# A fused three-block transformer forward on one core: the first norm's root moved behind the first layer, and the last down projection and norm done by token

## The reference, cut to what matters

```python
def rms_norm(x, g):
    xf = x.astype(jnp.float32)
    y = xf * lax.rsqrt(jnp.mean(xf * xf, axis=-1, keepdims=True) + RMS_EPS)
    return y.astype(x.dtype) * g

# first block, layer 0 (the start of the kernel)
hn = rms_norm(h, mix_norm_g[0])
u = hn @ w_pw1 + b_pw1                      # 1024 -> 2048
a, gate = jnp.split(u, 2, axis=-1)
u = a * jax.nn.sigmoid(gate)
u = depthwise_causal_conv(u, w_dw) + b_dw   # 31 taps
u = jax.nn.silu(layer_norm(u, ln_g, ln_b))
h = h + u @ w_pw2 + b_pw2
...
# third block (the end of the kernel)
hf = rmsnorm(x, norm_ffn_g[l])
gate, up = jnp.split(hf @ w_ffn_in[l], 2, axis=-1)      # 1024 -> 2 x 2816
x = x + (jax.nn.silu(gate) * up) @ w_ffn_out[l]         # 2816 -> 1024
return rmsnorm(x, final_norm_g)
```

## Time and profile before

| | |
|---|---|
| Median of 3 runs | 2007.54 us (2007.24 to 2014.68) |
| The profiled execution: its own time | 2004.65 us |
| Its span, first to last instruction | 2002.8 us |
| TensorE busy | 1962.8 us, 98% |
| VectorE busy | 1529.3 us, 76% |
| ScalarE busy | 1214.5 us, 61% |
| Mean granted clock of TensorE | 0.994 |

### The profile page before, as it was taken

The page is one execution under the profiler, slowest core; times in us unless marked ns, Lnnn a source line. Parts: engine busy times, 40 slices in busy tenths (PEclk is TensorE's granted clock), DMA queues, the critical chain, the costliest instruction groups (busy, mean ns, idle before and its releaser), DMA issues.

```text
span 2002.8 us, 32075 instructions
## 1 busy us (share of the span) xinstructions
PE 1962.8 (98%) x12418; PEld 1736.1 (87%) x12418; DVE 1529.3 (76%) x1656; ACT 1214.5 (61%) x1297; POOL 64.2 (3%) x105
## 2 busy tenths in 40 slices
PE   8999999999999999999999999999999999999997
PEld 7799998688888888888888888889988889999997
DVE  7776554889998999899989988996486568776662
ACT  4264443777777777777877778774354555545442
POOL 3020000000000000000000000001000100030000
PEclk8999999999999999999999999999999999999999
DMA  6635453499999999999999999984532434454551
GB/s 253 176 127 183 175 191 125 149 363 373 355 372 363 365 373 356 372 366 366 371 357 373 359 371 364 363 330 149 197 108 96 148 107 151 165 185 174 189 189 43
DMA packets 75865, 510.26 MB, mean 255 GB/s; under 512 B 8320, under 2 KB 14464, under 8 KB 14592
## 3 DMA queue, kind: packets, MB, share of 16 engines
q1 hardware_dynamic: 75776, 508.98, 68.2%
HBM read 506.66 MB, written 2.29 MB: 254 GB/s over the span
## 4 chain that ended last, share of the span: by engine, by line
PE 88%; DVE 5%; ACT 2%; issue 2%; DMA 2%; POOL 1%; SPq 0%; ACTq 0%; DVEq 0%; POOLq 0%
PE ps L924 9%; PE ps L928 9%; PE ps L656 9%; PE ps L927 9%; PE ps L659 9%; PE ps L660 9%; PE ps L949 5%; PE ps L953 5%; PE ps L952 5%; PE ps L1224 2%; PE ps L1226 2%; PE ps L1227 2%; PE ps L1150 1%; PE ps L935 1%; PE ps L685 1%
## 5 line engine op out<-in xcount | busy, mean ns | idle before, releaser
L1973 DVE TENSOR_TENSOR ring_r<-ring,high 128x2048 fp32r<-128x2048 f32 x227 | 517.4, 2289 | 53.6 <-ACT high L1612 31.8
L1612 ACT ACTIVATE high<-ring 128x2048 fp32r<-128x2048 f32 x224 | 428.7, 1914 | 14.1 <-DMA ring<-w_stream 13.0
L1846 DVE TENSOR_TENSOR ring_r<-ring,high 128x2048 fp32r<-128x2048 f32 x126 | 288.8, 2296 | 118.9 <-ACT high L1415 118.5
L927 PE MATMUL ps<-ring_r,big_r 128*128 128x512 f32 x896 | 349.0, 390 | 0.0
L659 PE MATMUL ps<-scr_r,high 128*128 128x256 f32 (+1 forms) x1200 | 343.3, 286 | 0.0
L1415 ACT ACTIVATE high<-ring 128x2048 fp32r<-128x2048 f32 x126 | 239.5, 1907 | 163.6 <-PE ps L656 89.2
L1973 DVE TENSOR_TENSOR ring_r<-ring,scr_r 128x2048 fp32r<-128x2048 f32 x112 | 256.3, 2288 | 39.3 <-ACT scr_r L1612 39.0
L656 PE MATMUL ps<-sq_r,high 128*128 128x272 f32 (+1 forms) x832 | 239.0, 287 | 5.0 <-DVE scr_r L1864 5.0
L660 PE MATMUL ps<-sq_r,ring_r 128*128 128x272 f32 (+1 forms) x832 | 238.5, 287 | 0.0
L659 PEld LDWEIGHTS ps<-scr_r,high 128*128 128x128 f32 x1200 | 227.9, 190 | 0.2
L1612 ACT ACTIVATE scr_r<-ring 128x2048 fp32r<-128x2048 f32 x112 | 214.5, 1915 | 16.8 <-DMA ring<-w_stream 16.8
(11 more groups left out here) (503 smaller groups left out, 3922.9 us busy)
## 6 DMA issues: line engine op xcount, KB each, us to landing
ring<-w_stream SPq DMA_DIRECT2D x477, 1024.0 KB, 4.8
big<-spread SPq DMA_DIRECT2D x32, 146.0 KB, 3.0
spread<-big SPq DMA_DIRECT2D x8, 151.0 KB, 5.0
h<-h_in SPq DMA_DIRECT2D x1, 1088.0 KB, 5.1
out<-hn SPq DMA_DIRECT2D x1, 1024.0 KB, 4.7
vec<-vec_in SPq DMA_DIRECT2D x1, 576.0 KB, 8.2
```

The lines of the kernel that those rows point to most:

```text
L927: pe.matmul(o, x_item_high[:, k, :], w_low[:, cols], start=False, stop=False)
L1612: act.activation(w_high, w, ACT.Copy).then_inc(S["moe_high"], 1)
L1846: dve.tensor_tensor(w_low, blocks_at(c, 0, CH), w_high.bitcast(F32), ALU.subtract).then_inc(S["weights_low"], 1)
L1973: dve.tensor_tensor(w_low, w, w_high.bitcast(F32), ALU.subtract).then_inc(S["moe_low"], 1)
```

## The change

It has three parts. At the start, the products of the first layer take h times the gain without the root; the sum of squares is made behind pair 0, and VectorE multiplies both tiles of every pair by the reciprocal root when it takes them out of PSUM (`glu_scaled`). Chunk 0 is loaded and split in two halves, the gain of the first norm is loaded ahead of h, four of the eight squares are VectorE's, and in VectorE's loop `make_diag` stands ahead of conv_u and the weight split behind the taps. At the end, the down projection has tokens on the partitions: hidden tiles are stationary, 512 weight columns move, x enters through 16 products with the identity, and the norm is done by token with ScalarE's accumulating squares, and the result goes out in four transfers. In between, four layers count on one semaphore, `pair_done`.

```diff
 SyncE
-            sp.dma_start(h[:, :, :], h_in).then_inc(S["h_landed"], 16)
-            for c in range(RING):
-                sp.dma_start(slot(c), w_stream[c]).then_inc(dense_landed[c], 16)
-                if c == 0:
-                    sp.dma_start(vec[:, :], vec_in).then_inc(S["vec_landed"], 16)
+            half = CH * WIDE // 2
+            sp.dma_start(slot(0)[:, 0:half], w_stream[0][:, 0:half]).then_inc(S["first_landed"], 16)
+            sp.dma_start(vec[:, 0:KD], vec_in[:, 0:KD]).then_inc(S["h_landed"], 16)
+            sp.dma_start(h[:, :, :], h_in).then_inc(S["h_landed"], 16)
+            sp.dma_start(slot(0)[:, half:], w_stream[0][:, half:]).then_inc(dense_landed[0], 16)
+            sp.dma_start(vec[:, KD:], vec_in[:, KD:]).then_inc(S["vec_landed"], 16)
+            for c in range(1, RING):
+                sp.dma_start(slot(c), w_stream[c]).then_inc(dense_landed[c], 16)
...
-            sp.wait_ge(S["normed"], normed_at(10, 7))
-            sp.dma_start(out, hn256).then_inc(S["out_done"], 16)
-            sp.wait_ge(S["out_done"], 16)
+            sp.wait_ge(S["pair_done"], 5 * KD)
+            sp.dma_start(out_gain, gain_in).then_inc(S["vec_landed"], 16)
+            for t in range(2):
+                sp.wait_ge(S["out_scaled"], t + 1)
+                sp.dma_start(out[t][:, 0:512], out_tok[:, t, 0:512]).then_inc(S["out_done"], 16)
+                sp.wait_ge(*out_step(t, 3))
+                sp.dma_start(out[t][:, 512:], out_tok[:, t, 512:]).then_inc(S["out_done"], 16)
+            sp.wait_ge(S["out_done"], 64)
 TensorE
-            keep_busy(5, 6)
-            sum_tiles(0, T0, range(KD))
             keep_busy(6, 6)
-            pe.wait_ge(S["consts_ready"], 2)
-            pe.wait_ge(S["vec_landed"], 16)
...
-                bank_owner[b] = (S["glu_done"], j + 1)
-                bank_owner[b + 1] = (S["glu_sig"], j + 1)
+                bank_owner[b] = bank_owner[b + 1] = (S["glu_scaled"], j + 1)
+                if j == 0:
+                    pe.wait_ge(S["sq_ready"], KD)
+                    for k in range(KD):
+                        mm = pe.matmul(ps[:, 7, 0:T0], ones[:, 0:P], hn[:, k, :], start=(k == 0), stop=(k == KD - 1))
+                    mm.then_inc(S["sum_done"], 1)
...
+            def out_products(k, w_high, w_low, t, half, first=False):
+                rows, cols = slice(t * P, (t + 1) * P), slice(512 * half, 512 * (half + 1))
+                o = ps[:, out_bank(t, half), :]
+                begun(first, pe.matmul(o, hid_high[:, k, rows], w_high[:, cols], start=False, stop=False))
+                pe.matmul(o, hid_high[:, k, rows], w_low[:, cols], start=False, stop=False)
+                return pe.matmul(o, hid_low[:, k, rows], w_high[:, cols], start=False, stop=(k == KF - 1))
+            def out_by_token(b_out):
+                for t in range(2):
+                    for half in range(2):
+                        claim(out_bank(t, half))
+                    for k in range(KD):
+                        pe.matmul(ps[:, out_bank(t, k // 4), k % 4 * P:(k % 4 + 1) * P], x[:, k, t * P:(t + 1) * P],
+                                  ident[:, :], start=(k % 4 == 0), stop=False)
+                for k in range(KF - 2):
+                    pe.wait_ge(S["ffn_hid"], KF + k + 1)
+                    _, _, first = parts_of(b_out + 4 * k)
...
+                    for t in range(2):
+                        for half in range(2):
+                            out_products(k, w_high, w_low, t, half, first and t == 0 and half == 0)
...
+                for t in range(2):
+                    for half in range(2):
+                        for n in range(2):
...
+                            mm = out_products(KF - 2 + n, w_high, w_low, t, half, first and t == 0 and half == 0 and n == 0)
+                        mm.then_inc(S["ffn_down"], 1)
 ScalarE
-            norm(0, h, T0, lambda k: None)
-            split_weights(0)
+            act.wait_ge(S["first_landed"], 16)
+            split_first(0)
+            act.wait_ge(S["h_landed"], 32)
             for k in range(KD):
-                if k == 3:
-                    split_weights(1)
-                act.wait_ge(S["normed"], normed_at(0, k))
-                act.activation(sq_r[:, k, :], hn[:, k, :], ACT.Copy).then_inc(S["input_high"], 1)
+                if k == KD // 2:
+                    wait_landed(act, 0, None)
+                    split_first(1)
+                act.activation(sq_r[:, k, :], h[:, k, :], ACT.Copy, scale=vcol("mix_g0", k)).then_inc(S["input_high"], 1)
+            for k in range(KD // 2):
+                act.activation(hn[:, k, :], h[:, k, :], ACT.Square).then_inc(S["sq_ready"], 1)
+            split_weights(1)
+            root(1, T0, eps_col)
...
-            norm(10, x, SEQ, lambda k: act.wait_ge(S["ffn_out"], 8 + k + 1))
+            act.activation(warm, eps_col, ACT.Sqrt)
+            for t in range(2):
+                for half in range(2):
+                    act.wait_ge(S["ffn_down"], KD + 2 * t + half + 1)
+                    if half == 0:
+                        act.wait_ge(*out_step(t, 0))
+                    squared = act.activation(out_squares[:, 2 * t + half, :], ps[:, out_bank(t, half), :], ACT.Square, scale=1.0 / 32,
+                                             accum_out=out_sum[:, t, half:half + 1])
...
+                act.wait_ge(*out_step(t, 1))
+                act.activation(out_std[:, t, 0:1], out_sum[:, t, 1:2], ACT.Sqrt, bias=out_eps[:, t, 0:1])\
+                   .then_inc(S["std_ready"], 1)
+                act.wait_ge(*out_step(t, 2))
+                act.activation(out_tok[:, t, 0:512], out_gained[:, t, :], ACT.Copy, scale=out_root[:, t, 0:1])\
+                   .then_inc(S["out_scaled"], 1)
 VectorE
-            norm(0, h, hn, "mix_g0", T0, first_block=0, low=in_low0)
+            split_first(0)
+            dve.wait_ge(S["h_landed"], 32)
+            for k in range(KD):
+                if k == KD // 2:
+                    split_first(1)
+                input_low(h, k, vcol("mix_g0", 0, 8), T0, sq_r, in_low0)
+            for k in range(KD // 2, KD):
+                dve.tensor_tensor(hn[:, k, :], h[:, k, :], h[:, k, :], ALU.mult).then_inc(S["sq_ready"], 1)
+            split_weights(1)
...
+            inverse_root(0, T0)
...
             for j in range(8):
-                split_weights((BOFF["pw1"] + j * KD + KD - 1) // CH + LOOK)
+                dve.wait_ge(S["pair_done"], 2 * j + 2)
+                dve.tensor_tensor(gu[:, j % 2, :, :], ps[:, 2 * (j % 3):2 * (j % 3) + 2, 0:T0], times_root(T0), ALU.mult)\
+                   .then_inc(S["glu_scaled"], 1)
+                make_diag(j)
+                if j == 0:
+                    split_weights(2)
                 dve.wait_ge(S["glu_sig"], j + 1)
-                dve.scalar_tensor_tensor(out=conv_u[:, j, CONVW - 1:CONVW - 1 + T0], in0=ps[:, 2 * (j % 3), 0:T0],
-                                         scalar=vcol("b_pw1", j), in1=gate_sb[:, j % 2, :],
+                dve.scalar_tensor_tensor(out=conv_u[:, j, CONVW - 1:CONVW - 1 + T0], in0=gu[:, j % 2, 0, :],
+                                         scalar=vcol("b_pw1", j), in1=gu[:, j % 2, 1, :],
                                          op0=ALU.add, op1=ALU.mult).then_inc(S["glu_done"], 1)
                 last_taps(j)
-                make_diag(j)
+                split_weights((BOFF["pw1"] + j * KD + KD - 1) // CH + LOOK)
                 if j >= 3:
                     take_conv(j - 3)
...
-            norm(10, x, hn, "final3_g", SEQ)
+            for t in range(2):
+                dve.wait_ge(S["ffn_down"], KD + 2 * t + 1)
+                dve.tensor_tensor(out_gained[:, t, :], ps[:, out_bank(t, 0), :], out_gain[:, 0:512], ALU.mult)\
+                   .then_inc(S["normed"], 1)
+                dve.wait_ge(S["sq_ready"], 8 * 10 + t + 1)
+                dve.tensor_scalar(out_eps[:, t, 0:1], out_sum[:, t, 0:1], EPS, None, ALU.add).then_inc(S["normed"], 1)
+                dve.wait_ge(S["std_ready"], 10 + t + 1)
+                dve.reciprocal(out_root[:, t, 0:1], out_std[:, t, 0:1]).then_inc(S["normed"], 1)
+                dve.wait_ge(*out_step(t, 2))
+                dve.scalar_tensor_tensor(out=out_tok[:, t, 512:], in0=ps[:, out_bank(t, 1), :], scalar=out_root[:, t, 0:1],
+                                         in1=out_gain[:, 512:], op0=ALU.mult, op1=ALU.mult).then_inc(S["normed"], 1)
```

More of the change, by code:

```diff
@@ L182, in highs_made, with lows_made @@
 def highs_made(n):
-    return n + sum(c in HALVED for c in SPLIT_CHUNKS[0:n])
+    return n + sum(c in HALVED for c in SPLIT_CHUNKS[0:n]) + (n > 0)
+def lows_made(n):
+    return n + (n > 0)
 def half_due(s, behind):
@@ L204, in moba_slope, with program @@
     return float(np.float32(2.0 ** (-8.0 * (2 * h + 2) / 16)))
-def program(nc, w_stream, vec_in, h_in, out):
+def program(nc, w_stream, vec_in, h_in, gain_in, out):
     with ExitStack() as ctx:
@@ L261, in program @@
         diagonal = scr[:, 4352:4384]
```

(33 more changed lines are left out.)

95 lines of the change are left out of this document (51 added, 44 removed).

## The result

The changed kernel took 2024.02 us in the median (2020.54 to 2030.4, 5 runs), the kernel before 2007.54 us in the same session (2006.37 to 2014.68, 5 runs): ratio 1.0079, 95% interval 1.0063 to 1.0094. It is slower by 16 us, and outside the predicted range of 1996 to 2010. The profiled execution took 2024.02 us with a span of 2022.3, against 2004.65 and 2002.8 before: 19.5 us of span to be explained.

A forecast was written before the change was run, and what follows sets the result against it. TensorE, busy 98% of the span, was taken as the bound, with VectorE's backlog the limit up to 57 us. Front +4.3 and tail -7.3 gave -3.0 on the 2007.54 median: 2004.5 us, range 1996 to 2010.

The forecast's parts named there:

- the order of VECS ... cost nothing further: Front: the new order of VECS, with chunk 0's halves, conv_sum's place and moved splits, was to add no time.
- Slower by over 0.5%: Whole kernel: outcome at least 10 us slower, expected only from a clock staying low at its worst; chance 0.04.
- The root T: First layer: time at which the root is written, taken as 20.0 us, with 19.4 and 22.2 as bounds.
- From T to take_conv(0): Front: VectorE's work from the root's writing to the first convolution sum's end, 35.0 us, ending at 55.0.
- VectorE's backlog doesn't bind: Front: rival in which TensorE keeps its whole 7.9 us lead, total -15.2, 1992.3 us; chance 0.17.
- Gap and clock: Ahead of conv_tile(1): TensorE idles about 8 us, clock returns at 0.50, tile of 2.96 us takes about 5; +2.2.
- The clock holds: Front: rival with the clock unreduced through both gaps, front +1.5, tail -7.3, 2001.7 us; chance 0.17.
- The other side's rival: Front: clock stays at 1.2 GHz after the gap, front +7.7, total +0.4, 2007.9 us, worst 2014; chance 0.14.
- The closed loop: Convolution stage: make_diag waits for a tile needing VectorE's later take_conv; 10.4 us a round against 9.57, three rounds +2.5.
- The last tile: Convolution stage's end: conv_tile(7) starts 11.7 us after conv_tile(4) instead of 10.3, behind late shifted loads; +1.4.
- The end: Last down projection and norm by token: TensorE -1.2, behind the last product 6.3 for 12.4 us, together -7.3.
- One semaphore for four layers: Layers counting on pair_done: changes thresholds only, no time.

The follow-up runs named there:

- e1: Changed kernel with 8 unused float32 columns (32 bytes) behind vec, so later buffers lie where they did before the change; 2005.70 us, ratio 0.9988.
- e9: Kernel before with 512 bytes of padding behind vec; 2006.40 us, ratio 0.9995.
- e8: e1 with VectorE's first loop reordered: take_conv(j - 3) ahead of the sigmoid wait, later diagonals behind the taps; 1995.5 us, ratio 0.9955.
- e7: Kernel before with only the edit of the end and the gain's row, at the old addresses; 1998.72 us, ratio 0.9956.
- e2: Kernel before with 8 unused columns (32 bytes) behind vec, no instruction changed; 2021.08 us, ratio 1.0067.
- e5: Kernel before with 128 bytes of padding behind vec; 2018.46 us, ratio 1.0060.
- e6: Kernel before with ring, high and vec 32 bytes higher and all buffers behind vec 128 bytes higher; 2026.72 us, ratio 1.0101.
- e12: e8 with h and gains asked for first, first two input parts ahead of the half chunk's split, four more idle products; 1994.88 us, ratio 0.9931.

## Why the prediction was wrong

**The failed step** is a half sentence: "the order of VECS ... cost nothing further". I read it as a change of offsets inside vec and not as a length that places every buffer behind it. Slower by over 0.5% had 0.04, and for another mechanism. The runs showed in its place that those 32 bytes lengthen the 512-column products: eight items of +2.1 us are 17 of the 18.2 us in the middle, and the 264 products of the end another 1.7 us. With this step put right (e1), the changed kernel takes 2005.7 us, inside the range and 1.2 from the forecast. But that closeness is partly luck, since two terms missed in opposite directions: in e1's trace the front costs 7.5 us where I had 4.3, and the end gives 8.3 where I had 7.3.

**The root T.** Taken as 20.0, measured 22.9, beyond the bound of 22.2. Each part was off: h let ScalarE begin at 9.3, not 7.25 (I gave the queue's full rate to what was asked for first. Two things were otherwise. By 9.3 us, 252 GB/s x 9.3 us = 2.3 MB had come, more than the 1.6 MB of the pieces up to h, so those asked for later were sharing the rate. And from 3 to 5 us, while the half chunk and the gains came, the windows show 197 and 218 GB/s, where the kernel before had 426 and 400 with h; why is open). Copy to first product took 1.18, as taken. Pair 0 took 8.1 us and not 6.4, since the clock was 0.50 behind 4.6 us of idle time; I had set 2.0 us of idle time, too small mostly through h's error, and had the low clock only in the bound. That 2.0 us leave the clock alone was read from a single row; in e9, with the same code as before, 1.9 us did not. Sums and root were as taken.

**From T to take_conv(0): 35.0 predicted, 35.1 measured** (22.9 to 58.03). VectorE's backlog is the bound up to there, as read; the rival "VectorE's backlog doesn't bind" was wrong for this order and came true in part in e8, whose order takes the sum out of the backlog's way. conv_tile(1) moved by +1.2 rather than -1.8, all of the difference being T's.

**Gap and clock: +2.2 predicted, +2.2 measured** (5.18 us for a tile of 2.96, behind 7.6 us with hardly any work). "The clock holds" was wrong at both gaps. The other side's rival took the clock to stay low for 8 us or more; it was back at 1.00 within 5.

**The closed loop: 10.4 predicted, 10.48 measured**, three rounds +2.8 for +2.5. The wait of make_diag in front of conv_u is real, 2.53 us each round, and e8, which takes it away, returns to 9.55.

**The last tile: +1.4 predicted, +1.8 measured.** 1.2 + 2.2 + 2.8 + 1.8 = 8.0.

**The end: -7.3 predicted, -6.7 measured, -8.3 at the old addresses (e7).** Behind the last product it was 6.0 for 12.7, so -6.7 for -6.1. TensorE's part, from the last scaling to the start of the last product, was 64.7 before and after, and 63.0 in e7 (1935.68 to 1998.68): nothing and -1.7, where I had -1.2. The 16 products with the identity took 3.5 us for 4.1, which is the rest of that. The spacing of the wide products, taken as 0.227 from the earlier trace rows, was 0.234 in the changed kernel and 0.227 in e1: the row was right for the addresses it came from. The Trainium skill, page "TensorE: Matmul & The Clock Gate", section "Back-to-back issue gap", gives 216 ns for a single isolated product of 512 columns by its formula; the stream of products here reaches that at neither distance.

**One semaphore for four layers** cost nothing that shows: e1 has the same item as the kernel before, from the start of the last item to the last scaling it takes 704.3 us (1235.5 to 1939.80) for 704.4, and from conv_tile(7) to the first item the changed kernel takes 282.5 us for 282.1.

## What to carry to other kernels

A change that alters the length of one buffer moves all buffers behind it. Compare addresses before and after, and pad so that they stay; if identical code gets slower with no new wait and an unchanged clock, look at the mean duration of each form of product before looking for a mechanism. When an engine's order holds a wait for a product whose own start needs a later instruction of that engine, work out the closed loop and move the releasing instruction ahead of the work (here 12 us of the trace for a few lines). And a head start won on one engine is worth nothing until the engine with the backlog gets through it: count from there.

## What the runs showed of the hardware

- A product of 512 fp32r columns takes 0.227 to 0.229 us from start to start when the buffers of the loaded tile and of the moving operand keep their distance of the kernel before or are moved against each other by 256 or 512 bytes, and 0.232 to 0.236 when they are moved by 32, 64, 96 or 128 bytes. The exception that stays open is scr with big, which went from 391 to 393 or 394 ns in e2, e5 and e6 without a change of their distance. Which address both have makes no difference (all +128, all +384). Products of 256 and 272 columns show none of it (48 of the convolution stage's in 6.01 us after and before, by the mean step). What in the memory causes it no run here shows. The Trainium skill, page "SBUF — State Buffer", section "Operand start alignment", asks only for starts at a multiple of the element's size; all kernels here keep to that, and it says nothing of time.
- The granted clock was 0.50 behind idle spells of TensorE of 2.5 us (e12), 3.6 (e8), 4.6 and 7.6 (the changed kernel), and back at 1.00 some 3 to 5 us after its work began, where the 1.2 GHz stretch of the kernel before lasted from 16.8 to 25.3 us. But the length of a spell does not settle it. Ahead of conv_tile(1) the clock stayed at 1.00 behind 2.0 us in the kernel before and behind 3.4 us in e7, and was 0.50 behind 1.9 us in e9, where the tile took 4.64 us instead of 2.96. A forecast has to carry both levels.
- Of transfers asked for one behind the other on one queue the first did not get all that was moved: 1088 KB of h took 7.6 us to land behind 516 KB, with 0.7 MB of later ones come by then, and 5.1 when it was asked for first.
